# First modulation of a two-layer trunk built in halves of the model dimension, with one ordered queue for the large loads

## What is computed

```python
c_act = jax.nn.silu(c)
mod = c_act @ ada_w[i] + ada_b[i]                  # ada_w[i]: (1024, 6144)
sh1, sc1, g1, sh2, sc2, g2 = jnp.split(mod[:, None, :], 6, axis=-1)
h = rms_norm(x, norm_mix[i]) * (1.0 + sc1) + sh1
y = dilated_attention(h, w_qkv, ...)               # layer 0: w_qkv (1024, 9216)
x = x + g1 * y
```

## Time and profile before

| | us |
|---|---|
| profiled execution, span from first to last instruction | 910.1 |
| median of three runs | 909.22 |
| TensorE busy | 847.7 |
| VectorE busy | 623.6 |
| ScalarE busy | 426.3 |
| GpSimd (POOL) busy | 119.3 |

### The profile page before, as it was taken

How to read it: one execution, slowest core, us unless ns; L and a number is a source line. 1 busy time by engine, 2 the same in 40 slices (tenths; PEclk the granted TensorE clock), 3 DMA queues, 4 the chain that set the end, 5 groups by cost and what they waited for, 6 DMA issues and landing times.

```text
span 910.1 us, 10752 instructions
## 1 busy us (share of the span) xinstructions
PE 847.7 (93%) x4195; PEld 709.3 (78%) x4195; DVE 623.6 (69%) x749; ACT 426.3 (47%) x515; POOL 119.3 (13%) x159
## 2 busy tenths in 40 slices
PE   1599999999999979999999979999989799999997
PEld 0477888889888858888888857888877588888886
DVE  5879678677686767766777775895774754454543
ACT  3255446545455355333433446658554553433431
POOL 4101001010010010111111100462620000000000
PEclk9999999999999999999999979999979899999999
DMA  9899766876767627889889835444224175555541
GB/s 339 284 271 310 240 224 214 274 222 231 230 221 243 190 89 249 286 277 316 283 278 318 294 109 182 139 139 139 93 93 139 46 225 191 185 185 185 185 139 46
DMA packets 119607, 188.96 MB, mean 208 GB/s; under 512 B 5580, under 2 KB 90758, under 8 KB 119558
## 3 DMA queue, kind: packets, MB, share of 16 engines
q1 hardware_dynamic: 105350, 137.90, 47.4%
q0 software_dynamic: 14208, 50.39, 15.9%
HBM read 187.18 MB, written 1.09 MB: 207 GB/s over the span
## 4 chain that ended last, share of the span: by engine, by line
PE 81%; DVE 8%; DMA 4%; ACT 3%; issue 2%; SPq 2%; DVEq 0%; ACTq 0%
PE bank L390 69%; PE bank L659 2%; PE bank L508 2%; PE bank L484 2%; DMA raw<-in_attn_w_qkv_dram 1%; DVE wlo L1052 1%; PE bank L469 1%; PE bank L604 1%; ACT arena L774 1%; PE bank L434 1%; SPq L268 1%; PE bank L406 1%; DMA arena<-in_distance_table_dram 1%; DMA bias_rows<-arena 1%; DMA ada_w<-in_ada_w_dram 1%
## 5 line engine op out<-in xcount | busy, mean ns | idle before, releaser
L1052 DVE TENSOR_TENSOR wlo<-raw,whi 128x2048 fp32r<-128x2048 f32 x126 | 288.7, 2291 | 126.6 <-ACT whi L724 126.3
L390 PE MATMUL bank<-whi,hT_hi 128*128 128x512 f32 (+1 forms) x800 | 315.7, 395 | 8.7 <-DVE hT_lo L1145 8.3
L724 ACT ACTIVATE whi<-raw 128x2048 fp32r<-128x2048 f32 x126 | 241.5, 1916 | 150.3 <-PE bank L390 120.5
L390 PE MATMUL bank<-whi,hT_lo 128*128 128x512 f32 (+1 forms) x800 | 308.5, 386 | 0.0
L390 PE MATMUL bank<-wlo,hT_hi 128*128 128x512 f32 (+1 forms) x800 | 308.0, 385 | 0.0
L390 PEld LDWEIGHTS bank<-whi,hT_hi 128*128 128x128 f32 x800 | 152.7, 191 | 42.6 <-DVE hT_lo L1145 10.1
L390 PEld LDWEIGHTS bank<-whi,hT_lo 128*128 128x128 f32 x800 | 152.4, 191 | 30.4
L390 PEld LDWEIGHTS bank<-wlo,hT_hi 128*128 128x128 f32 x800 | 152.8, 191 | 28.8 <-issue 1.0
L1077 DVE SCALAR_TENSOR_TENSOR acc<-ada_w,cact,acc 128x1024 f32<-128x1024 f32 x80 | 102.3, 1279 | 25.0 <-DMA ada_w<-in_ada_w_dram 24.6
L390 PE MATMUL bank<-whi,oT_hi 128*128 128x512 f32 x240 | 97.4, 406 | 3.6 <-DVE oT_lo L1430 1.6
L312 POOL DMA_DIRECT2D ada_w<-in_ada_w_dram x80 | 42.6, 532 | 408.3 <-DVE acc L1077 408.3
(11 more groups left out here) (137 smaller groups left out, 734.0 us busy)
## 6 DMA issues: line engine op xcount, KB each, us to landing
raw<-in_ffn_w_dram SPq DMA_DIRECT2D x88, 512.0 KB, 4.9
ada_w<-in_ada_w_dram POOLq DMA_DIRECT2D x80, 512.0 KB, 5.2
raw<-in_attn_w_qkv_dram SPq DMA_DIRECT2D x64, 512.0 KB, 4.8
raw<-in_ffn_w_dram SPq DMA_DIRECT2D x22, 1024.0 KB, 6.0
raw<-in_hgrn_w_in_dram SPq DMA_DIRECT2D x16, 1024.0 KB, 5.4
arena<-in_ada_w_dram POOLq DMA_DIRECT2D x16, 512.0 KB, 6.6
raw<-in_attn_w_qkv_dram SPq DMA_DIRECT2D x4, 1024.0 KB, 5.1
raw<-in_attn_w_out_dram SPq DMA_DIRECT2D x4, 1024.0 KB, 6.0
```

What stands on the lines that cost most here:

```text
L390: mm = nc.tensor.matmul(d[:, 0:n], l, r[:, k, cut], start=first and k == 0 and q == 0, stop=last and k == nk - 1 and q == 2)
L724: return nc.scalar.activation(dst, src, ACT.Copy)
L1052: nc.vector.tensor_tensor(wlo[:, m % SPL, :], raw[:, m % RAW, :], fp(whi[:, m % SPL, :]), ALU.subtract).then_inc(s["split"], 1)
```

## The change

Block 0 of the first modulation becomes the first 512 columns of both the shift and the scale, block 1 the second 512. With block 0, kc 0 to 3 of h are finished, and `half_unit` multiplies them by three units: the first contraction halves of chunks 0, 1 and 2 (for pair 0 the order of units is `ORDER0`, and chunk 2 has banks 4 and 5). Their second halves are units 3, 4 and 5. Block 1 is summed between the two token tiles of unit 2. Chunks 0, 1 and 2 are then complete after units 3, 4 and 5, and their normalisations stand at units 4, 5 and 6 (`qk_last`), their transposes after units 5, 6 and 7 (`qk_sets`); k goes through bank 7.

SP's queue carries c, all sixteen first tiles of `ada_w`, x and the units in one order; POOL's queue has block 0's bias row, the small rows, the tables and block 1's bias row, then the later tiles of `ada_w`, the first of which waits for all sixteen first products. The bias rows are written after unit 4 and loaded with units 6 and 7; the pair masks are loaded with unit 20. First products are whole (1024 columns) instead of two halves. ScalarE copies the table, scales x and copies the transposes from PSUM into hT ahead of the modulation; affine operations then work in place. The lower bounds' sigmoid moves to layer 1. The 36 products beside units 0 to 35 now lie beside units 3 to 35 (`ada_done`), block 2's sums still after units 9 and 10. The scale columns 0 to 7 of `cols` become free, c has a tile of its own, and the half products' semaphore goes.

```diff
 
             if m < M_OUT0:
                 pr, j = divmod(m, QU)
+                j = ORDER0[j] if pr == 0 else j
                 w = a["attn_w_qkv"][0]
...
+            def first_ada(n):
+                blk, k = divmod(n, KC)
+                if n >= FIRST:
+                    sp.wait_ge(s["ada_used"], n - FIRST + 1)
+                sp.dma_start(first_w[n % FIRST].rearrange("p (w c) -> p w c", w=2),
+                             halves(a["ada_w"][0, k * P:(k + 1) * P, :], blk)).then_inc(first_in[n % FIRST], 16)
+
+            def load_unit(m):
                 if m >= RAW:
                     sp.wait_ge(s["split"], m - RAW + 1)
                 for src, nk, c0, n in pieces(m):
                     slot = raw[:, m % RAW, :].rearrange("p (k n) -> p k n", k=nk)
                     sp.dma_start(slot[:, :, c0:c0 + n], src).then_inc(raw_in[m % RAW], 16)
-                if m == 2:
-                    sp.dma_start(masks[:], a["pair_masks"]).then_inc(s["masks_in"], 16)
+
+            sp.dma_start(crow[:], a["c"].rearrange("a (k d) -> (a k) d", d=P)).then_inc(s["c_in"], 16)
+            for n in range(2):
+                first_ada(n)
+            sp.dma_start(x[:], a["x"][0].rearrange("(t p) d -> p t d", p=P)).then_inc(s["x_in"], 16)
+            for n in range(2, KC):
+                first_ada(n)
+            load_unit(0)
+            load_unit(1)
+            for n in range(KC, KC + 2):
+                first_ada(n)
+            load_unit(2)
+            for n in range(KC + 2, KC + 6):
+                first_ada(n)
+            load_unit(3)
+            for n in range(KC + 6, 2 * KC):
+                first_ada(n)
+            for m in range(4, UNITS):
+                load_unit(m)
+                if m == 4:
                     sp.wait_ge(s["tab_cp"], 1)
                     sp.dma_start(scratch, tabT).then_inc(s["tab_out"], 16)
+                if m == 5:
+                    sp.wait_ge(s["ada_used"], 2 * KC)
+                if m in (6, 7):
                     sp.wait_ge(s["tab_out"], 16)
-                    load_bias(sp, 0)
-                    load_bias(sp, 1)
+                    load_bias(sp, m - 6)
+                if m == 20:
+                    sp.dma_start(masks[:], a["pair_masks"]).then_inc(s["masks_in"], 16)
                 for h in range(2, HEADS):
...
 
         def chunk_end(n):
 
+            if n < 3:
+                return 4 + n
             pr, c = divmod(n, 5)
             return pr * QU + (2 * c + 2 if c < 4 else 9)
 
+        def chunk_bank(n):
+
+            return 4 if n == 2 else 2 * (n % 2)
+
         def blocks_of(qt):
             return [(g, kt) for g in range(NG) for kt in range(qt + 1)]
...
+
+        def qk_sets(m):
+
+            pr, j = divmod(m, QU)
+            if pr == 0:
+                return [(j - 5, which) for which in range(2)] if 5 <= j <= 7 else []
+            return [(3 * pr + (j - 3) // 2, (j - 3) % 2)] if pr < PAIRS and 3 <= j <= 8 else []
+
+        def qk_last(m):
+
+            pr, j = divmod(m, QU)
+            first = 3 if pr == 0 else 1
+            step = 1 if pr == 0 else 2
+            n, odd = divmod(j - first, step)
+            return 3 * pr + n if pr < PAIRS and odd == 0 and 0 <= n < 3 else None
 
...
+            def half_unit(m, half, tiles):
+                n = m % 3
+                b = chunk_bank(n)
+                for t in tiles:
+                    pe.wait_ge(s["xn_lo"], 2 * half + t + 1)
+                    unit(m, hT_hi, hT_lo, 4, 4 * half, 512, [[bank[b]], [bank[b + 1]]], half == 0, half == 1, tiles=(t,))
+
+            pe.wait_ge(s["cact_s"], 1)
+            pe.wait_ge(s["cols_s"], 1)
+            half_unit(0, 0, (0, 1))
             pe.wait_ge(s["tab_cp"], 1)
+            half_unit(1, 0, (0, 1))
+            pe.wait_ge(s["h0_raw"], 4)
+            half_unit(2, 0, (0,))
+            reduce_task(1)
+            half_unit(2, 0, (1,))
...
                 pr, j = divmod(m, QU)
                 n = 5 * pr + min(j // 2, 4)
-                if j % 2 == 0 and n >= 2:
+                if j % 2 == 0:
                     c = (n - 2) % 5
                     if c < 3:
                         pe.wait_ge(s["qk_norm"], 3 * ((n - 2) // 5) + c + 1)
                     else:
                         pe.wait_ge(s["v_ev"], 2 * ((n - 2) // 5) + c - 2)
-                b = 2 * (n % 2)
+                b = chunk_bank(n)
                 nk, w = (8, 256) if j == 8 else (4, 512)
                 unit(m, hT_hi, hT_lo, nk, 0 if j == 8 else 4 * (j % 2), w, [[bank[b]], [bank[b + 1]]],
                      j % 2 == 0, j % 2 == 1 or j == 8)
...
-            nc.scalar.activation(cact[:], cols[:, 0:KC], ACT.Silu).then_inc(s["cact_s"], 1)
-            act.wait_ge(s["lbd_s"], 1)
-            nc.scalar.activation(lb[:, 0, :], lbd[:], ACT.Sigmoid).then_inc(s["lb_s"], 1)
+            act.wait_ge(s["c_t"], 1)
+            nc.scalar.activation(cact[:], bank[0][:, 0:KC], ACT.Silu).then_inc(s["cact_s"], 1)
             nc.scalar.preload_act_table_set("natural_log_exp_and_others")
             for t in range(T):
                 norm_stats(0, t)
+            act.wait_ge(s["tab_mm"], 1)
+            copy(tabT, bank[2][0:GH, 0:TABLE]).then_inc(s["tab_cp"], 1)
+            act.wait_ge(s["newton"], 3)
+            for t in range(T):
+                nc.scalar.activation(xn[:, t], x[:, t], ACT.Copy, scale=small[:, 2 + t:3 + t]).then_inc(s["xn_s"], 1)
+            for t in range(T):
+                for g in range(2):
+                    act.wait_ge(s["xn_tr"], 2 * t + g + 1)
+                    copy(hT[:, 4 * g:4 * g + 4, t * P:(t + 1) * P],
+                         bank[4 + 2 * t + g][:].rearrange("p (k t) -> p k t", k=4)).then_inc(s["h0_raw"], 1)
+
+            def first_round(half, t):
+
+                cut = slice(t * P, (t + 1) * P)
+                first = 4 * half + 2
+                for kc in range(first, 4 * half + 4):
+                    i = nc.scalar.activation(hT[:, kc, cut], hT[:, kc, cut], ACT.Identity, bias=mod_b[:, 0, 0, kc:kc + 1],
+                                             scale=mod_a[:, 0, 0, kc:kc + 1])
+                i.then_inc(s["h0_aff_s"], 1)
+                act.wait_ge(s["h0_aff_s"], 2 * half + t + 1)
+                act.wait_ge(s["h0_aff"], 2 * half + t + 1)
+                copy(hT_hi[:, 4 * half:4 * half + 4, cut], hT[:, 4 * half:4 * half + 4, cut]).then_inc(s["xn_hi"], 1)
+
             round_unit(0)
-            norm_round(0, 0)
+            act.wait_ge(s["h0_raw"], 4)
+            act.wait_ge(s["ada_ev"], 1)
+            first_round(0, 0)
+            first_round(0, 1)
             round_unit(1)
-            norm_round(0, 1)
+            round_unit(2)
+            round_unit(3)
+            act.wait_ge(s["ada_ev"], 2)
+            first_round(1, 0)
+            first_round(1, 1)
...
+            def first_affine(half, t):
+
+                cut = slice(t * P, (t + 1) * P)
+                for kc in range(4 * half, 4 * half + 2):
+                    i = nc.vector.tensor_scalar(hT[:, kc, cut], hT[:, kc, cut], mod_a[:, 0, 0, kc:kc + 1],
+                                                mod_b[:, 0, 0, kc:kc + 1], ALU.mult, ALU.add)
+                i.then_inc(s["h0_aff"], 1)
+
+            def first_rest(half, t):
+
+                dve.wait_ge(s["xn_hi"], 2 * half + t + 1)
+                v = lambda y: y[:, 4 * half:4 * half + 4, t * P:(t + 1) * P]
+                nc.vector.tensor_tensor(v(hT_lo), v(hT), fp(v(hT_hi)), ALU.subtract).then_inc(s["xn_lo"], 1)
+
+            for blk in range(2):
+                nc.vector.memset(acc[:, blk], 0.0).then_inc(s["ada_zero"], 1)
             dve.wait_ge(s["cact_s"], 1)
-            dve.wait_ge(s["ada_zero"], 1)
-            for n in range(2 * KC):
+            for n in range(KC):
                 ada_op(n)
                 if n == 1:
-                    dve.wait_ge(s["tab_mm"], 1)
-                    nc.vector.tensor_copy(tabT, bank[1][0:GH, 0:TABLE]).then_inc(s["tab_cp"], 1)
-                if n in (4, 5):
-                    norm_scale(0, n - 4)
-                if n == 12:
-                    ada_evac(0, 3)
+                    dve.wait_ge(s["cols_t"], 1)
+                    nc.vector.tensor_copy(cols[:, NORM0:NORM0 + NROWS], bank[1][:, 0:NROWS]).then_inc(s["cols_s"], 1)
+                    dve.wait_ge(s["cols_s"], 1)
+                    nc.vector.tensor_scalar(cols[:, GAIN0:GAIN0 + NG], cols[:, GAIN0:GAIN0 + NG], float(P) ** -0.5,
+                                            None, ALU.mult).then_inc(s["cols_s"], 1)
+                    nc.vector.tensor_tensor(lbd[:], cols[:, LB0 + KC:LB0 + 2 * KC], cols[:, LB0:LB0 + KC],
+                                            ALU.subtract).then_inc(s["lbd_s"], 1)
+                if n == 3:
+                    dve.wait_ge(s["xn_rstd"], 2)
+                    refine(small[:, 2:4], small[:, 0:2], 2, 4, 1.0 / D)
             split_unit(0)
-            ada_evac(1, 3)
+            ada_evac(0, 3)
+            dve.wait_ge(s["ada_ev"], 1)
```

(105 more changed lines are left out.)

124 lines of the change are left out of this document (60 added, 64 removed).

## The result

Over 20 runs each, the changed kernel took 911.20 us in the median and the kernel before 908.56. The ratio is 1.0027, with a 95% interval from 1.0016 to 1.0038: slower by 2.5 us, a little, but clear of the uncertainty. I had forecast 4.0 us less (905.2), so the sign was wrong; 911.2 lies above the 903 to 907.5 of the sum and just outside the 901 to 911 that was to hold in eight cases of ten. The change is inside the 0.5% that I called no change.

What follows compares the result with a forecast made beforehand. TensorE was taken as the bound, except where it cannot start. Unit 9 6.5 us earlier, less a 2.5 us wait, gave 4.0 off the 909.22 median: 905.2 us, range 903 to 907.5, eight in ten between 901 and 911.

Steps and rivals of the forecast that it cites:

- unit 9 as the landmark: Unit 9's start, 99.76 us before the change, moves the end by as much, less later additions; forecast at 93.3.
- S: Moment when unit 0's weights are in, rounded and split, and the evacuations done: 26.3 us, between 24.2 and 28.5.
- the second chain through the table: Small tables, table matmul, ScalarE's copy, scaling of x, transposes: scaling expected at 14.5 to 16.5 us, deciding only after 16.1.
- The new wait ahead of unit 6: TensorE waits about 5.5 us, until 73.2, for chunk 1's normalisation to free banks 2 and 3; half clock adds 1.6.
- 2.5 us wait ahead of block 2's row sum: At unit 9 TensorE waits once for block 2's eighth product, behind the first attention maximum on VectorE: 2.5 us.
- The forecast's own sign of being wrong: Forecast is wrong if no pause stands ahead of unit 6, or if unit 9 is early and the end is not.
- part 2: VectorE's fixed order of products, splits, sums and normalisations from S on, ending with chunk 1's normalisation at S+46.9.
- this 1.6 only as a bound (4.1): Upper bound for TensorE's wait ahead of block 2's row sum: 4.1 us with a low clock behind it, 2.5 taken.
- D: Rival, 10%: small loads on POOL's queue land late, delaying the start; 910.2 us, or 913.1 at 13.4 us after issue.
- A: Rival, 25%: the pause ahead of unit 6 costs less, third product's transfer in time and clock held; 901.9 to 903.6 us.
- B: Rival, 13%: bytes bind at 280 to 320 GB/s, product weights in 1.5 to 2 us later than VectorE wants; 908.9 us.
- C: Rival, 7%: the low clock behind the pause ahead of unit 6 lasts 10.2 us, costing 3.2 more; 908.4 us.

Runs made afterwards that it cites:

- banks: Changed kernel with the bank parity of chunks from 3 on turned round, so unit 6 waits for chunk 0's normalisation, not chunk 1's: 906.44 us, ratio 0.9972.
- normalisation first: Changed kernel with VectorE's normalisation of a chunk put ahead of the late product in units 0 to 8: 908.81 us, ratio 0.9981.
- bias later: Changed kernel with the second load of bias rows moved from unit 7 to unit 11 in SP's queue: 908.77 us, ratio 0.9995.
- bias source: Changed kernel with the second bias rows loaded from x in the same place, so head 1's bias is wrong: 909.58 us, ratio 0.9996.
- the first experiment: Changed kernel with later products respread so block 2's eighth lies beside unit 8, not unit 9: 908.04 us, ratio 0.9989.
- the first three and the last: Changed kernel with block 2's product early (908.04 us), second bias load at unit 11 (908.77), banks turned round (906.44); these three plus normalisation ahead of the product (896.16).

## Why the prediction was wrong

*What held.* Where the bound lies; unit 9 as the landmark; and the price of the parts up to 60 us, to 1.3 us in sum. S, predicted at 26.3, is the evacuation that ends at 26.9. Unit 0's weights were in at 22.5 (21.4 predicted), and the second chain through the table was ahead of them:

```profile
15.12 0.48 ACT L806 ACTIVATE arena<-bank 24x383 f32<-24x383 f32 x1 [1.43 <-PE bank L503]
15.84 2.19 ACT L870 ACTIVATE arena<-x,small 128x1024 f32<-128x1024 f32 x2 [0.24 <-DVE small L1216]
...
22.50 1.91 ACT L806 ACTIVATE whi<-raw 128x2048 fp32r<-128x2048 f32 x1 [1.16 <-DMA raw<-in_attn_w_qkv_dram]
```

The new wait ahead of unit 6, its cause (banks 2 and 3 and chunk 1's normalisation) and the half clock behind it (1.6 foreseen, 1.7 measured in unit 6) were foreseen, and so was the 2.5 us wait ahead of block 2's row sum, which measured 2.6. The experiments with the banks and the early product show both as causes. The wait was foreseen as one of 5.5 us; it came as two, 4.7 ahead of chunk 0's transposes and 4.4 ahead of unit 6. The forecast's own sign of being wrong came true: unit 9 was 1.6 us early and the end was not.

*The step that failed* is in part 2: "The third product finds a transfer issued only when the first of its two buffers was used; 1.7 of waiting." The waiting measured 5.2, and it began 1.3 us later than foreseen (S gives 0.6 of that), so the product started at 68.4 and not at 63.6. By the sum the landing had some 6.3 us: the first product done at S+31.0, the third started at S+37.3. It took 9.55, because the second bias rows now stand in SP's queue just ahead of it. The DMA view of the changed kernel, 60 to 62 us and 64 to 66:

```profile
DMA packets 267, 0.27 MB, mean 133 GB/s; under 512 B 8, under 2 KB 267, under 8 KB 267
...
q1 hardware_dynamic: 267, 0.27, 96.0%
```

```profile
DMA packets 458, 0.82 MB, mean 408 GB/s; under 512 B 9, under 2 KB 342, under 8 KB 458
...
q0 software_dynamic: 124, 0.48, 58.2%
q1 hardware_dynamic: 334, 0.34, 48.0%
```

In the first stretch the engines are busy to 0.96 of their time and move 133 GB/s, all of it SP's queue; POOL's queue, issued at 58.79, moves nothing yet. In the second 408 GB/s flow and POOL's queue has 58% of the time. In the kernel with the late bias load POOL's transfer also had its first packets only some 3 us after its issue (5 in the changed kernel), but what SP had queued drained at 368 GB/s meanwhile, here from 58 to 60 us:

```profile
DMA packets 734, 0.74 MB, mean 368 GB/s; under 512 B 16, under 2 KB 734, under 8 KB 734
...
q1 hardware_dynamic: 734, 0.74, 109.0%
```

The experiments with the load moved and with its source changed show the cause. I had a row for it and misread it: the 280 GB/s of the earlier trace rows I took for the price of 1 KB packets. In that stretch of the kernel before, the second of the two bias loads was still under way. They were issued at 44.5 and 44.9 and landed after 5.1 and 8.5 us, at 49.6 and 53.4. In the same window the rate climbs from some 200 GB/s to over 380 as the second one ends (40 slices of 49 to 54 us):

```profile
DMA to landing us min/median/max: 5.1/6.8/8.5
GB/s 238 279 246 270 270 221 221 246 180 172 213 221 197 229 254 205 205 238 238 262 270 279 229 295 319 295 303 262 328 270 344 320 377 385 393 393 393 385 385 385
```

All its packets are under 2 KB, the fast ones at the end as well. I took the one slow stretch for a property of packet size, and never priced the bias loads that the change put in VectorE's way. Nor had it a place among the rivals, whose chances with the forecast's own (45, 25, 13, 7 and 10) left nothing for what I had not thought of.

The late landing is the largest term, not the only one: with the load moved, unit 11 starts 1.8 us earlier than in the kernel before, not 4.0.

The Trainium skill (Perfetto Trace Analysis, DMA Optimizations) puts a significant overhead on transfers under 2 KB. The runs support that far less than I wrote: 1 KB packets reach 368 GB/s, 4 KB ones 410. Unit 0 was in at 22.5 us, not at the 20 to 21 that I had worked out by that rule. The section speaks of small transfers, and these are transfers of 512 KB in small packets; to read it of packets was mine.

*A second term was missing.* Behind the 2.6 us wait at unit 9 the clock fell to half: the row sum took 1.19 instead of 0.86 and unit 10 6.99 instead of 5.47. I had this 1.6 only as a bound (4.1) and left it out; the nearest row, a pause of 1.85 us that kept the clock, spoke for that. It is no fixed price: five profiles have this wait at 2.6 us, and unit 10 took 6.99, 7.06 and 6.13 us behind it in three (the changed kernel, normalisation first, banks) and 5.46 and 5.48 in two (bias later, bias source). How often the changed kernel's runs pay it no profile tells.

*The price of half clock.* The 0.455 us a matmul that I gave would mean 50% lost; the 47% in the sum fits the 0.43 at which those matmuls follow each other. Either gives 1.6 to 1.7 us.

The sum, then, by landmarks: unit 9 at 98.2 against 93.3 foreseen (4.8 of the 4.9 are there at unit 6's start, 78.0 against 73.2: 3.5 of waiting for the weights and the 1.3 ahead of it), and 1.8 for the clock at unit 10. That is 6.7 of the 6.8 us between -4.0 and the +2.8 at unit 11.

*The rivals.* D fell: the table was in at 13.6 us, 5.7 after its issue, and the scaling of x began at 15.84, inside the 14.5 to 16.5 foreseen. The rule of the Trainium skill cited for it (DMA: Bandwidth & Descriptors, Queues, rings and completion order: each engine goes round between the queues that have work) fits this, with the small loads in POOL's queue and SP's full. It does not explain the 3 to 5 us in which POOL's transfer had been issued and moved nothing beside SP's; whether its descriptors were ready then no view shows. A and B had no part in it: the pause cost more, and the bytes were in time but for 1.1 us at unit 0. Of C the length was right and the price was not: half clock lasts some 10 us (0.68 in the mean from 66.9 to 78, 0.50 from 78 to 81), but 7 of them lie ahead of unit 6, in the pauses and the transposes between them, where TensorE waits for VectorE anyway; unit 6 loses 1.7.

## What to carry to other kernels

A head start on one engine is worth only what the next engine can keep up with: here three chunks finished in a row, each with a sum and a normalisation at every unit instead of every second, made VectorE's order the bound, and a few lines on who waits behind whom (banks, order, one load) turned +0.3% into -1.5%. When a transfer is moved, price it by a stretch in which it is under way, and compare with a stretch of the same packets without it: a low GB/s at full engines may belong to one of the transfers under way, and the mean of the view doesn't say to which. Check each sum or copy that follows an even spread of work for the one place where rounding puts its last input behind it.

## What the runs showed that I had not expected

A load of 384 rows of 1 KB, starting 4 bytes apart in a 36 KB table of DRAM, kept the engines busy to 0.96 for 2 us at 133 GB/s and made another queue's transfer land some 3 us later; as many bytes from x, in packets of 3 KB, did not. And a sum over partitions that takes 16 matmuls of one column can be followed by half clock with hardly a pause (0.3 us) ahead of it: in the first experiment block 3's sum ends at 227.8, in the kernel before at 230.1, with the same instructions around it. The windows behind the two:

```profile
227.80:231.20 3.40, 3.40 (x10) 2.63 (x10) 2.46 (x2) 0.83 (x1) 0.00 (x0) 0.52 1.06 244
```

```profile
230.10:235.70 5.60, 5.60 (x26) 4.65 (x26) 2.46 (x2) 0.86 (x1) 0.00 (x1) 1.00 0.98 292
```

In the profiles of four of the eight experiments (the first three and the last) the distance to the kernel before shrinks by 1.6 or 1.7 us at that unit; I found no cause for which kernels pay it.
